# Sum of squares of x for the RMS norm factor: eight strip products on TensorE replaced by three adds on VectorE and one product with ones

## The chip, the cores and the metric

One Trainium2 chip (trn2), one of its NeuronCores. The metric is the device time of one execution in microseconds (us); for several executions their median is given. TensorE multiplies matrices and writes PSUM, VectorE (DVE in the rows) and ScalarE (ACT) do elementwise work, SyncE (SP) starts the DMAs that bring the weights. The engines run side by side and wait for one another through semaphores; each works through its own instructions in program order.

## The reference, cut to what matters

Two transformer blocks (`l` = 0, 1) are followed by a modulated attention and retention layer and a mixture of experts. All is float32, 256 tokens of width 1024. In each of the two blocks an RMS norm stands at three places:

```python
def rms_norm(x, g):
    xf = x.astype(jnp.float32)
    y = xf * lax.rsqrt(jnp.mean(xf * xf, axis=-1, keepdims=True) + EPS)
    return (y * g.astype(jnp.float32)).astype(x.dtype)
...
    for l in range(DEPTH):
        h = rms_norm(x, norm_g[l, 0])
        x = x + 0.5 * swiglu(h, ffn_w_gate[l, 0], ffn_w_up[l, 0], ffn_w_down[l, 0])
        h = rms_norm(x, norm_g[l, 1])
        proj = h @ w_in[l]
        ...
        h = rms_norm(x, norm_g[l, 2])
        x = x + 0.5 * swiglu(h, ffn_w_gate[l, 1], ffn_w_up[l, 1], ffn_w_down[l, 1])
```

The change is about how `jnp.mean(xf * xf)` is formed at these six places (two blocks with three norms each).

## The kernel before

x is held turned: `xT` has 128 partitions, eight tiles (`KD`), and 256 tokens in each. A tile is 128 of the 1024 features, so the sum over features runs over eight tiles and over the 128 partitions. The products with x don't wait for the norm: they take x times the gain, rounded into `hh` (high part) and `hl` (rest), and the result is multiplied afterwards with the factor 1/rms of each token (`rstd`). A weight comes in pieces of 128x1024 by DMA into `W`; ScalarE makes its high part `WH` (L1522), VectorE its rest `WL` (L1907), four pairs in rotation (`PAIRS`), and TensorE makes three products for each 128x128 weight (`mm3`, L799, recorded at L780).

The norm factor is made while TensorE already works at the first two blocks of the products. ScalarE squares x into `mT` (L1545, four instructions of two tiles). TensorE, after the first block of products (the gate block of an FFN, or block c = 0 of the projection), does `squares_by_strip` (L872): each of the eight tiles of squares is multiplied with 32 columns of ones, tile k into the strip of 32 partitions at k % 4 * 32 of PSUM bank 0, so that four strips each hold the sum of two tiles. ScalarE copies the strips to `rs` (`strips_out`, L1548, recorded at L1551). TensorE, after the second block of products, does `squares_of_strips` (L881): ones times `rs`, which adds all partitions; every row of a strip counts 32 times, hence the scale 1/(32 D). ScalarE takes the root (`root`, L1553, recorded at L1556), VectorE the reciprocal (`norm_factor`, L1958, recorded at L1961), and then the results of the first blocks are multiplied with it.

The order of the work around this is written out by hand, engine by engine, and fixed when the kernel is built:

- TensorE, `ffn` (L936) at b = 0: gate products, strips, up products, product of the strips, then block 1. The projection (L1003 on) does the same with c = 0, c = 1 and c = 2.
- ScalarE: `used(2)` (L1525) makes the high parts of the pieces due next; in `ffn` (L1624) two such calls, `strips_out` and `root` stand ahead of the first Silu.
- VectorE: `used(2)` (L1910) makes the rests; in `ffn` (L2145) and in the projection (L2210 on) two such calls stand ahead of `norm_factor` at b = 0 or c = 0.

A piece may be split ahead of its use by three pieces, as far as a pair is free:

```python
                while may_split(st["split"], st["used"], free, ahead):
                    n = st["split"]
                    dve.wait_ge(high_ready, n + 1)
                    ...
                    v.tensor_tensor(low, W[:, i % RAW, :], high.bitcast(F32), ALU.subtract).then_inc(low_ready, 1)
```

With pieces 0 and 1 for the first block of products and 2 and 3 for the second, the first `used(2)` reaches piece 4 and the second one piece 6. Piece 6 takes the pair of piece 2, so its high part waits (`pair_used`) until TensorE is in the second half of the second block.

`link` (L1895) lets a VectorE instruction count a semaphore up and has VectorE wait for it, so that the next one reads finished data.

Of the kernel before, what the change touches and what calls it, by code (L numbers as in the profile page):

```python
# [8 lines left out]
ALU = mybir.AluOpType  # L9
ACT = mybir.ActivationFunctionType  # L10
# [8 lines left out]
T = 256  # L19
# [259 lines left out]
def build(nc, I, out):  # L279
    ctx = ExitStack()  # L280
    with ctx:
# [492 lines left out]
        def _(pe):  # L774
# [94 lines left out]
                       f == 0, f == 1, then=work_ready if f else None)  # L869
                turns.step()  # L870

            def squares_by_strip():  # L872

                for k in range(KD):
                    if k % 2 == 0:
                        pe.wait_ge(sq_ready, due(sq_ready))
                    at = k % 4 * 32
                    mm(ps[at:at + 32, 0, 0:T], ones[:, 0:32], mT[:, k, :], k < 4, k >= 4,
                       then=sum_ready if k == KD - 1 else None)

            def squares_of_strips():  # L881

                pe.wait_ge(part_ready, due(part_ready))
                mm(ps[:, 1, 0:T], ones[:, :], rs[:, :], True, True, then=sum_ready)

# [50 lines left out]
            def ffn(l, i):  # L936

                for b in range(FF_BLOCKS + 1):
                    if b < FF_BLOCKS:
                        two_tiles("ffn_gate", begin(), h_wait=b == 0, then=work_ready)  # L940
                        turns.step()
                        if b == 0:
                            squares_by_strip()
                        two_tiles("ffn_up", begin(), then=work_ready)
                        turns.step()
                        if b == 0:
                            squares_of_strips()
                    if (l, i, b) == (0, 0, LATE_BLOCK):
                        late_vectors()
                    if ada_unit(l, i, b) is not None:  # L950
                        if ada_unit(l, i, b) == 0:
                            pe.wait_ge(act_setup, 3)
                        if ada_unit(l, i, b) < SUMMED_FROM:
                            ada_rows(ada_unit(l, i, b))
                    if ada_unit(l, i, b - 1) is not None:
                        ada_columns(ada_unit(l, i, b - 1))
                    if (l, i, b) == (1, 1, CONTEXT_AT + 1):
                        turn_context()
                    if (l, i, b) == (1, 1, CONTEXT_AT + 2):
                        pe.wait_ge(lrow_ready, 1)  # L960
                        bank = begin()
                        mm(bank[:, 0:40], ones[0:1, :], lrow[:, :], True, True, then=work_ready)
                        turns.step()
                    if 0 < b < FF_BLOCKS:
                        c = b - 1
                        pe.wait_ge(hid_ready, due(hid_ready))
                        for f in range(2):
                            w = take("ffn_down")
                            hid = at((hid_h[:, c % 2, :], hid_l[:, c % 2, :]), f * T, T)
                            for n in range(KD):  # L970
                                mm3(ps[:, n // 2, (n % 2) * T:(n % 2 + 1) * T], at(w, n * P), hid,
                                    c == 0 and f == 0 and n % 2 == 0, False)
                            done_pair()
                pe.wait_ge(hid_ready, due(hid_ready))
                c = FF_BLOCKS - 1
                ws = [take("ffn_down") for f in range(2)]
                for n in range(KD):
                    for f in range(2):
                        hid = at((hid_h[:, c % 2, :], hid_l[:, c % 2, :]), f * T, T)
                        mm3(ps[:, n // 2, (n % 2) * T:(n % 2 + 1) * T], at(ws[f], n * P), hid, False, f == 1,  # L980
                            then=acc_ready if f and n % 2 == 1 else None)
                done_pair(2)
# [20 lines left out]
            for l in range(DEPTH):  # L1003
                ffn(l, 0)
                proj = {}
                for c in range(15):
                    bank = begin()
                    if c not in (4, 5, 10, 11, 14):
                        two_tiles("w_in", bank, h_wait=c == 0, then=work_ready)
                    else:  # L1010

                        for half in range(2):
                            w = take("w_in")
                            for j in range(4):
                                k = 4 * half + j
                                end = k == KD - 1
                                if c == 14:
                                    mm3(bank[:, 0:T], at(w, j * 256), h_at(k), k == 0, end)
                                n, v0 = (P, T) if c == 14 else (256, 0)
                                for tt in range(TT):  # L1020
                                    mm3(bank[:, v0 + tt * n:v0 + (tt + 1) * n], h_at(k, tt * P, P),
                                        at(w, j * 256 + 256 - n, n), k == 0 and tt == 0 and c != 14, end,
                                        then=work_ready if end and tt else None)
                            done_pair()
                    proj[c] = turns.step()
                    if c == 0:
                        squares_by_strip()
                    if c == 1:
                        squares_of_strips()
                    if c == 2:  # L1030
                        turn_factor(l)

# [470 lines left out]
        def _(act):  # L1503
# [41 lines left out]
                    nc.scalar.activation(mT[:, 2 * b:2 * b + 2, :], xT[:, 2 * b:2 * b + 2, :], ACT.Square)\  # L1545
                        .then_inc(sq_ready, 1)

            def strips_out():  # L1548

                act.wait_ge(sum_ready, due(sum_ready))  # L1550
                nc.scalar.activation(rs[:, :], ps[:, 0, 0:T], ACT.Copy).then_inc(part_ready, 1)  # L1551

            def root():  # L1553

                act.wait_ge(sum_ready, due(sum_ready))
                nc.scalar.activation(rs[:, :], ps[:, 1, 0:T], ACT.Sqrt, bias=eps[:, :], scale=1.0 / (32 * D))\  # L1556
                    .then_inc(rms, 1)

            def split_to(n):
# [64 lines left out]
            def ffn(l, i):  # L1624
                for b in range(FF_BLOCKS):
                    used(2)
                    if (l, i, b) == (0, 0, LATE_BLOCK + 1):
                        set_up()
                    if b == 0:
                        used(2)  # L1630
                        strips_out()
                        root()
                    act.wait_ge(work_free, turns.n + 1)
                    nc.scalar.activation(sg[:, b % 2, :], sg[:, b % 2, :], ACT.Silu).then_inc(sg_ready, 1)
                    turns.step()
                    if b:
                        used(2)
                    turns.step()
                    if (l, i, b) == (0, 0, LATE_BLOCK):
                        turns.step(LATE_TURNS)  # L1640
                    turns.step((ada_unit(l, i, b) is not None and ada_unit(l, i, b) < SUMMED_FROM) +
                               (ada_unit(l, i, b - 1) is not None))
                    if (l, i, b) == (1, 1, CONTEXT_AT):
                        context_root()
                    if (l, i, b) == (1, 1, CONTEXT_AT + 1):
                        round_context()
                        turns.step()
                    if (l, i, b) == (1, 1, CONTEXT_AT + 2):
                        turns.step()
                    if b:  # L1650
                        used(2)
                turns.step(ada_unit(l, i, FF_BLOCKS - 1) is not None)
                used(2, ahead=PAIRS - 2)
# [20 lines left out]
            for l in range(DEPTH):  # L1674
# [3 lines left out]
                for c in range(15):  # L1678
                    used(2)
                    act.wait_ge(work_ready, turns.n + 1)  # L1680
                    turns.step()
                    if c == 0:
                        strips_out()
                    if c == 1:
                        root()
                for s in range(MIX_STEPS):
# [184 lines left out]
        def _(dve):  # L1871
# [80 lines left out]
            def mixed_low(k):  # L1952
# [2 lines left out]
                v.tensor_tensor(mix_l[:, k, :], mT[:, k, :], mix_h[:, k, :].bitcast(F32), ALU.subtract)\  # L1955
                    .then_inc(mix_low, 1)

            def norm_factor():  # L1958

                dve.wait_ge(rms, due(rms))  # L1960
                v.reciprocal(rstd[:, :], rs[:, :]).then_inc(rstd_ready, 1)  # L1961
                dve.wait_ge(rstd_ready, due(rstd_ready))
# [182 lines left out]
            def ffn(l, i):  # L2145
                for b in range(FF_BLOCKS):
                    used(2)
                    if b == 0:
                        used(2)
                        norm_factor()  # L2150
                    bank = take()
                    give(v.tensor_tensor(by_two(sg[:, b % 2, :]), by_two(bank), factor_by_two(), ALU.mult))
# [57 lines left out]
            for l in range(DEPTH):  # L2210
# [4 lines left out]
                for c in range(15):  # L2215
# [3 lines left out]
                        used(2)  # L2219
                    if c == 0:  # L2220
                        used(2)
                        norm_factor()
                    bank = take()
                    if c == 4:
# [576 lines left out]
```

## Time and profile before

| | us |
|---|---|
| median of 3 runs | 1992.77 |
| lowest and highest | 1991.96, 1993.86 |
| profiled execution, its own time | 1993.51 |
| its span in the profile | 1991.7 |
| TensorE busy (matmuls) | 1940.5 (97%) |
| VectorE busy | 1223.4 (61%) |
| ScalarE busy | 703.2 (35%) |

The span runs from the first to the last instruction of the profiled execution; its own time is 1.8 us longer. Matmuls overlap in the pipeline, so that the distance from start to start is what one costs and not the duration in its row. The mean granted TensorE clock was 0.994 of full speed.

### The profile page before, as it was taken

The page shows a single profiled execution, that of the slowest core. Times are in us where ns is not written, and L with a number is a line of the kernel's source. Part 1 is how long each engine was busy: PE and PEld are TensorE (multiplying, and loading weights), DVE is VectorE, ACT ScalarE, POOL GpSimd, SP SyncE. Part 2 cuts the span into 40 slices and gives each one's busy share as a digit, 9 for nine tenths or more (in the row PEclk, how much of TensorE's full clock was granted, in tenths as well). Part 3 has the DMA queues.
Part 4 walks back from the last instruction along what each step waited for, and adds up shares of the span by engine and source line. Part 5 has one row for each costly group of instructions (what it writes and reads, how often), then busy time and mean ns, then how long its engine had stood idle before and what let it go on. Part 6 is the DMA issues. An engine that isn't in the chain of part 4 may idle for free.

```text
span 1991.7 us, 33632 instructions
## 1 busy us (share of the span) xinstructions
PE 1940.5 (97%) x14053; PEld 1598.8 (80%) x14053; DVE 1223.4 (61%) x2117; ACT 703.2 (35%) x1052; POOL 0.2 (0%) x4
## 2 busy tenths in 40 slices
PE   9999999999999999999999999999898999999997
PEld 9999998889999999999888999999665444434432
DVE  6665759877567877775987777757766333222221
ACT  5433536535334543353653534343332000000001
POOL 0000000000000000000000000000000000000000
PEclk9999999999999999999999999999899999999999
DMA  7798563276776677656325675654309999999996
GB/s 238 240 346 267 174 189 117 96 204 207 224 221 203 212 233 228 200 182 185 117 96 180 206 239 185 197 121 128 127 22 340 421 421 421 421 422 421 421 421 280
DMA packets 275282, 476.66 MB, mean 239 GB/s; under 512 B 29254, under 2 KB 235136, under 8 KB 250552
## 3 DMA queue, kind: packets, MB, share of 16 engines
q1 hardware_dynamic: 274876, 474.38, 68.9%
q8 instruction: 114, 1.87, 0.4%
q14 instruction: 40, 0.33, 0.1%
q10 hardware_dynamic: 252, 0.08, 0.0%
HBM read 473.27 MB, written 7.95 MB: 242 GB/s over the span
## 4 chain that ended last, share of the span: by engine, by line
PE 82%; DMA 11%; DVE 5%; ACT 1%; SPq 1%; issue 1%; DVEq 0%; ACTq 0%
PE ps L780 80%; DMA ring_over<-in_moe_w_up_dram 4%; DMA ring_zone<-in_moe_w_up_dram 3%; DMA hl_place<-in_moe_w_gate_dram 1%; DMA hl_place<-in_moe_w_up_dram 1%; DMA hT<-in_moe_w_up_dram 1%; SPq L700 1%; PE ps L1120 1%; PE ps L1263 0%; DVE PT L2353 0%; DVE WL L1978 0%; PE ps L1440 0%; DVE hl L1918 0%; ACT mT L1758 0%; ACT gT L1706 0%
## 5 line engine op out<-in xcount | busy, mean ns | idle before, releaser
L780 PE MATMUL ps<-hh,WH 128*128 128x256 f32 x2232 | 633.1, 284 | 1.3 <-DVE WL L1907 0.7
L780 PE MATMUL ps<-hl,WH 128*128 128x256 f32 x2232 | 622.9, 279 | 0.0
L780 PE MATMUL ps<-hh,WL 128*128 128x256 f32 x2232 | 622.9, 279 | 0.0
L1907 DVE TENSOR_TENSOR WL<-W,WH 128x1024 fp32r<-128x1024 f32 x390 | 471.6, 1223 | 244.0 <-ACT WH L1522 242.4
L1522 ACT ACTIVATE WH<-W 128x1024 fp32r<-128x1024 f32 x390 | 408.2, 1055 | 434.1 <-PE ps L780 398.2
L780 PEld LDWEIGHTS ps<-hh,WH 128*128 128x128 f32 x2232 | 418.8, 188 | 14.8 <-issue 11.6
L780 PEld LDWEIGHTS ps<-hl,WH 128*128 128x128 f32 x2232 | 418.7, 188 | 1.2 <-issue 1.0
L780 PEld LDWEIGHTS ps<-hh,WL 128*128 128x128 f32 x2232 | 418.8, 188 | 0.0
L780 PE MATMUL ps<-hid_h,WH 128*128 128x256 f32 x704 | 200.6, 285 | 0.0
L780 PE MATMUL ps<-hid_l,WH 128*128 128x256 f32 x704 | 197.6, 281 | 0.0
L780 PE MATMUL ps<-hid_h,WL 128*128 128x256 f32 x704 | 197.3, 280 | 0.0
L1838 ACT ACTIVATE sgE<-ps 128x512 f32<-128x512 f32 x16 | 9.6, 597 | 433.0 <-PE ps L780 433.0
L780 PEld LDWEIGHTS ps<-hid_h,WH 128*128 128x128 f32 x704 | 133.2, 189 | 3.5 <-issue 3.3
L2733 DVE TENSOR_TENSOR hidE<-sgE,ps 128x512 f32<-128x512 f32 x16 | 16.7, 1043 | 190.8 <-PE ps L780 190.8
L780 PEld LDWEIGHTS ps<-hid_l,WH 128*128 128x128 f32 x704 | 133.1, 189 | 0.0
L780 PEld LDWEIGHTS ps<-hid_h,WL 128*128 128x128 f32 x704 | 133.0, 189 | 0.0
L780 PE MATMUL ps<-yT,W 128*128 128x256 f32 x512 | 117.0, 381 | 0.8 <-DVE yT L2466 0.4
L780 PE MATMUL ps<-ring_over,XT 128*64 128x512 f32 x432 | 109.9, 594 | 6.7 <-DMA ring_over<-in_moe_w_up_dram 5.4
L780 PEld LDWEIGHTS ps<-yT,W 128*128 128x128 f32 x512 | 94.6, 190 | 15.7 <-issue 2.8
L780 PE MATMUL ps<-ring_zone,XT 128*64 128x512 f32 x336 | 89.1, 594 | 9.7 <-DMA ring_zone<-in_moe_w_up_dram 4.6
L780 PEld LDWEIGHTS ps<-ring_over,XT 128*64 128x64 f32 x432 | 37.6, 137 | 67.0 <-issue 66.9
L2750 DVE TENSOR_TENSOR yS<-ps,xT 128x512 f32<-128x512 f32 x32 | 22.1, 692 | 89.8 <-PE ps L780 89.8
(401 smaller groups left out, 2601.8 us busy)
## 6 DMA issues: line engine op xcount, KB each, us to landing
W<-in_ffn_w_gate_dram SPq DMA_DIRECT2D x88, 512.0 KB, 5.2
W<-in_ffn_w_up_dram SPq DMA_DIRECT2D x88, 512.0 KB, 4.8
W<-in_ffn_w_down_dram SPq DMA_DIRECT2D x88, 512.0 KB, 3.9
W<-in_w_in_dram SPq DMA_DIRECT2D x78, 512.0 KB, 4.6
ring_over<-in_moe_w_up_dram SPq DMA_DIRECT2D x28, 1024.0 KB, 26.5
ring_over<-in_moe_w_down_dram SPq DMA_DIRECT2D x28, 1024.0 KB, 26.2
ring_over<-in_moe_w_gate_dram SPq DMA_DIRECT2D x26, 1024.0 KB, 25.5
W<-in_w_gate_dram SPq DMA_DIRECT2D x48, 512.0 KB, 4.5
```

Of the source, the lines that this page charges most:

```text
L700: sp.dma_start(tile.rearrange("p (k n) -> p k n", k=src.shape[1]), src).then_inc(loaded, 16)
L780: ins = nc.tensor.matmul(o, lhsT, rhs, start=start, stop=stop, skip_group_check=True, **kw)
L1120: ins = nc.tensor.transpose(ps[:, TURN_BANK, k * T + q * P:k * T + (q + 1) * P], S[:, u % 4, q * T + k * P:q * T + (k + 1) * P], ident)
L1522: nc.scalar.activation(high, W[:, i % RAW, :], ACT.Copy).then_inc(high_ready, 1)
L1838: nc.scalar.activation(sgE[:, :], bank, ACT.Silu).then_inc(sg_ready, 1)
L1907: v.tensor_tensor(low, W[:, i % RAW, :], high.bitcast(F32), ALU.subtract).then_inc(low_ready, 1)
L2733: v.tensor_tensor(hidE[:, :].rearrange("p (k m) -> p m k", k=HIDDEN), by_row(sgE[:, :]), by_row(bank), ALU.mult).then_inc(work_free, 2)
L2750: give(v.tensor_tensor(yS[:, half * 512:(half + 1) * 512], bank, gate_rows[:, half * 512:(half + 1) * 512], ALU.mult))
```

## The change

VectorE adds the squares over the tiles in place in `mT`: 1024 columns (tiles 0 to 3 and 4 to 7), then 512, then 256 into `rs`. TensorE does the one product with ones, ScalarE takes the root with scale 1/D. Gone are the strip products and the copy of the strips. The adds stand on VectorE where `norm_factor` stood, directly ahead of it; the product stands on TensorE where `squares_of_strips` stood.

```diff
--- before.py
+++ after.py
@@ -869,17 +869,9 @@
                        f == 0, f == 1, then=work_ready if f else None)
                 turns.step()
 
-            def squares_by_strip():
-
-                for k in range(KD):
-                    if k % 2 == 0:
-                        pe.wait_ge(sq_ready, due(sq_ready))
-                    at = k % 4 * 32
-                    mm(ps[at:at + 32, 0, 0:T], ones[:, 0:32], mT[:, k, :], k < 4, k >= 4,
-                       then=sum_ready if k == KD - 1 else None)
-
-            def squares_of_strips():
-
+            def sum_of_squares():
+
+                due(sq_ready, 4)
                 pe.wait_ge(part_ready, due(part_ready))
                 mm(ps[:, 1, 0:T], ones[:, :], rs[:, :], True, True, then=sum_ready)
 
@@ -939,12 +931,10 @@
                     if b < FF_BLOCKS:
                         two_tiles("ffn_gate", begin(), h_wait=b == 0, then=work_ready)
                         turns.step()
-                        if b == 0:
-                            squares_by_strip()
                         two_tiles("ffn_up", begin(), then=work_ready)
                         turns.step()
                         if b == 0:
-                            squares_of_strips()
+                            sum_of_squares()
                     if (l, i, b) == (0, 0, LATE_BLOCK):
                         late_vectors()
                     if ada_unit(l, i, b) is not None:
@@ -1023,10 +1013,8 @@
                                         then=work_ready if end and tt else None)
                             done_pair()
                     proj[c] = turns.step()
-                    if c == 0:
-                        squares_by_strip()
                     if c == 1:
-                        squares_of_strips()
+                        sum_of_squares()
                     if c == 2:
                         turn_factor(l)
 
@@ -1545,15 +1533,10 @@
                     nc.scalar.activation(mT[:, 2 * b:2 * b + 2, :], xT[:, 2 * b:2 * b + 2, :], ACT.Square)\
                         .then_inc(sq_ready, 1)
 
-            def strips_out():
+            def root():
 
                 act.wait_ge(sum_ready, due(sum_ready))
-                nc.scalar.activation(rs[:, :], ps[:, 0, 0:T], ACT.Copy).then_inc(part_ready, 1)
-
-            def root():
-
-                act.wait_ge(sum_ready, due(sum_ready))
-                nc.scalar.activation(rs[:, :], ps[:, 1, 0:T], ACT.Sqrt, bias=eps[:, :], scale=1.0 / (32 * D))\
+                nc.scalar.activation(rs[:, :], ps[:, 1, 0:T], ACT.Sqrt, bias=eps[:, :], scale=1.0 / D)\
                     .then_inc(rms, 1)
 
             def split_to(n):
@@ -1628,7 +1611,6 @@
                         set_up()
                     if b == 0:
                         used(2)
-                        strips_out()
                         root()
                     act.wait_ge(work_free, turns.n + 1)
                     nc.scalar.activation(sg[:, b % 2, :], sg[:, b % 2, :], ACT.Silu).then_inc(sg_ready, 1)
@@ -1679,8 +1661,6 @@
                     used(2)
                     act.wait_ge(work_ready, turns.n + 1)
                     turns.step()
-                    if c == 0:
-                        strips_out()
                     if c == 1:
                         root()
                 for s in range(MIX_STEPS):
@@ -1955,6 +1935,14 @@
                 v.tensor_tensor(mix_l[:, k, :], mT[:, k, :], mix_h[:, k, :].bitcast(F32), ALU.subtract)\
                     .then_inc(mix_low, 1)
 
+            def sum_over_tiles():
+
+                dve.wait_ge(sq_ready, due(sq_ready, 4))
+                squares = flat(mT[:, :, :])
+                link(v.tensor_tensor(squares[:, 0:4 * T], squares[:, 0:4 * T], squares[:, 4 * T:8 * T], ALU.add))
+                link(v.tensor_tensor(squares[:, 0:2 * T], squares[:, 0:2 * T], squares[:, 2 * T:4 * T], ALU.add))
+                v.tensor_tensor(rs[:, :], squares[:, 0:T], squares[:, T:2 * T], ALU.add).then_inc(part_ready, 1)
+
             def norm_factor():
 
                 dve.wait_ge(rms, due(rms))
@@ -2147,6 +2135,7 @@
                     used(2)
                     if b == 0:
                         used(2)
+                        sum_over_tiles()
                         norm_factor()
                     bank = take()
                     give(v.tensor_tensor(by_two(sg[:, b % 2, :]), by_two(bank), factor_by_two(), ALU.mult))
@@ -2219,6 +2208,7 @@
                         used(2)
                     if c == 0:
                         used(2)
+                        sum_over_tiles()
                         norm_factor()
                     bank = take()
                     if c == 4:
```

## Rows read from the trace of the kernel before

**Rows 1.** The profile page: chain that ended last, shares of the span by engine

```profile
PE 82%; DMA 11%; DVE 5%; ACT 1%; SPq 1%; issue 1%; DVEq 0%; ACTq 0%
```

**Rows 2.** The same chain in order of time: start, us, what; two pieces

```profile
39.57 267.17 PE ps L780 x2296
...
426.14 527.08 PE ps L780 x4442
```

**Rows 3.** Timeline of TensorE around the strips (start, us, ...)

```profile
20.52 0.28 PE L780 MATMUL ps<-hh,WL 128*128 128x256 f32 x1
20.73 1.07 PE L780 MATMUL ps<-mT,ones 128*32 128x256 f32 x16
21.73 0.39 PE L780 MATMUL ps<-hh,WH 128*128 128x256 f32 x1
```

**Rows 4.** Timeline of TensorE around the product of the strips

```profile
27.49 0.59 PE L780 MATMUL ps<-rs,ones 128*128 128x256 f32 x2
```

**Rows 5.** Timeline of ScalarE in the same stretch

```profile
25.04 1.06 ACT L1522 ACTIVATE WH<-W 128x1024 fp32r<-128x1024 f32 x1 [2.54 <-PE ps L780]
...
26.39 1.28 ACT L1556 ACT_TABLE_LOAD   x1
```

**Rows 6.** Timeline of VectorE in the same stretch

```profile
26.13 1.23 DVE L1907 TENSOR_TENSOR WL<-W,WH 128x1024 fp32r<-128x1024 f32 x1 [2.37 <-ACT WH L1522]
28.63 1.75 DVE L1961 RECIPROCAL rstd<-rs 128x256 f32<-128x256 f32 x1 [1.27 <-ACT rs L1556]
...
31.88 0.69 DVE L2161 TENSOR_TENSOR S<-S 128x512 f32<-128x512 f32 x1 [0.17 <-ACT S L1634]
32.60 0.43 DVE L2162 CAST hid_h<-S 128x512 fp32r<-128x512 f32 x1
```

**Rows 7.** VectorE and TensorE at the second norm of block 0 (projection)

```profile
222.24 1.23 DVE L1907 TENSOR_TENSOR WL<-W,WH 128x1024 fp32r<-128x1024 f32 x1 [1.55 <-ACT WH L1522]
223.59 0.59 PE L780 MATMUL ps<-rs,ones 128*128 128x256 f32 x2
```

**Rows 8.** VectorE and TensorE at the last norm of block 1

```profile
1127.94 1.23 DVE L1907 TENSOR_TENSOR WL<-W,WH 128x1024 fp32r<-128x1024 f32 x1 [1.61 <-ACT WH L1522]
...
L780 PE MATMUL ps<-rs,ones x2: 378/378/378, 1129.3 to 1129.5; 128*128 128x256 f32 x2
```

**Rows 9.** Adds of 128x256 by tile: ns min/median/max, first and last start

```profile
L2275 DVE TENSOR_TENSOR mT<-mT,rs x32: 424/425/426, 411.6 to 1094.8; 128x256 f32<-128x256 f32 x32
```

**Rows 10.** The reciprocal's line, same columns

```profile
L1961 DVE RECIPROCAL rstd<-rs x6: 1752/1753/1754, 28.6 to 1130.4; 128x256 f32<-128x256 f32 x6
```

**Rows 11.** Timeline: TensorE waits for a rest made by VectorE

```profile
16.43 2.35 DVE L1907 TENSOR_TENSOR WL<-W,WH 128x1024 fp32r<-128x1024 f32 x2
...
17.71 0.39 PE L780 MATMUL ps<-hh,WH 128*128 128x256 f32 x1 [0.68 <-DVE WL L1907]
17.93 0.28 PE L780 MATMUL ps<-hl,WH 128*128 128x256 f32 x1
18.05 0.28 PE L780 MATMUL ps<-hh,WL 128*128 128x256 f32 x1
```

**Rows 12.** TensorE after three idle stretches, from the timeline

```profile
1233.45 1.23 PE L780 MATMUL ps<-WR,MOD 128*1 128x40 f32 x16 [4.37 <-DVE gT L2006]
...
1397.77 0.35 PE L780 MATMUL ps<-WH,hc_h 128*128 128x256 f32 x1 [2.33 <-DVE S L2370]
...
1543.92 0.66 PE L1440 MATMUL ps<-C,hidE 128*128 128x128 f32 x4 [3.06 <-DVE hidE L2733]
```

**Rows 13.** Windows of TensorE: stretch, sum, busy (instructions), granted clock, DMA share, GB/s

```profile
1234.00:1235.00 1.00, 1.00 (x13) 0.50 0.00 0
...
1239.00:1240.00 1.00, 1.00 (x10) 0.97 0.00 0
...
1395.00:1400.00 5.00, 2.67 (x21) 1.00 0.64 206
...
1545.00:1550.00 5.00, 4.34 (x22) 1.00 1.01 419
```

## The prediction, made before the changed kernel had run

> **What bounds the kernel now.** I read the chain that ended last first, then the same chain in order of time, then the timeline of each engine around one of the norms, and last the clock. The chain is TensorE for 82% of the span, and DMA for 11% [rows 1]. In order of time the stretches in which the six norms lie are unbroken TensorE: 267 us from 39.57 on and 527 us from 426.14 on [rows 2]. So what is taken from TensorE in these stretches is gained, and what TensorE has to wait for is lost; work of ScalarE or VectorE counts only where TensorE waits for it. The six norms are the six reciprocals [rows 10]. The profiled execution took 1993.51 us with a span of 1991.7 us; the median of the runs is 1992.77 us, and I add the difference worked out below to the median.
>
> **Removed from TensorE: the strips.** The last product before them starts at 20.52, the first after them at 21.73 [rows 3]; in an unbroken row they start 0.12 us apart, as at 17.93 and 18.05 [rows 11]. The strips cost 21.73 - 20.52 - 0.12 = 1.09 us. Six times that is 6.5 us off the path, the whole of what the change can gain. The copy of the strips on ScalarE is 0.4 us beside TensorE's work and is worth nothing: the load of the root's table that follows it starts at 26.39 and is done at 27.67, before the product of the strips has ended, and without the copy it only starts sooner [rows 4, 5]. In the projection the root stands behind a wait for the second block of products before and after, so nothing moves there.
>
> **Added on TensorE: nothing.** The product with ones and `rs` has the same shape as that of the strips and stands in the same place.
>
> **Added on VectorE: three adds, and where they stand.** This is the step that decides. The adds are ahead of the reciprocal and behind two `used(2)`, in VectorE's program order. The last rest made there is that of piece 6, and it runs from 26.13 to 27.36 [rows 6]. It can't be sooner: it waited 2.37 us for its high part, which started at 25.04 after waiting 2.54 us for TensorE, since piece 6 takes over the pair of piece 2 [rows 5, 6]. TensorE frees that pair as it enters the second half of the second block. So the start of this rest is tied to TensorE's own progress, and taking out the strips moves both sooner by the same 1.09 us. The squares have been ready for long (ScalarE's four squares lie before the strips), but the adds can't use that, as they stand behind this rest.
>
> TensorE reached the product of the strips at 27.49, 1.36 us after the start of that rest [rows 4, 6]. At the second norm it is 223.59 - 222.24 = 1.35 us [rows 7], at the last one 1129.3 - 1127.94 = 1.36 us [rows 8]; the other three read the same. All six are one case.
>
> No row shows an add of 128x1024 in place. The nearest is the rest itself, two inputs and 1024 columns: 1.23 us [rows 6]. For 512 columns it is L2161, 0.69 us [rows 6], for 256 the add of `mT` and `rs`, 0.425 us [rows 9]. They fit one line (0.266 us for 256 columns, 0.54 for 512), so I take them as they are. A pair of rests takes 2.35 us and not 2.46 [rows 11], so that an instruction with no wait on the one before it starts 1.13 us after that one's start: the first add starts at 26.13 + 1.13 = 27.26 on the old scale. Linked instructions start 32.60 - 31.88 = 0.72 us apart where the first one lasts 0.69 [rows 6], which is 0.03 for a link. The sum: 27.26 + (1.23 + 0.03) + (0.69 + 0.03) + 0.425 = 29.67. From the end of a rest, 16.43 + 1.23 = 17.66, to the product that waited for it, 17.71, is 0.05 [rows 11], so TensorE starts its product with ones at 29.72 in place of 27.49: it stands still for 2.23 us. Then it starts cold: 17.93 - 17.71 = 0.22 where it is otherwise 0.12 [rows 11], 0.10 more. In all 2.33 us lost.
>
> The Trainium skill (VectorE: DVE Perf Modes, The DRAIN you can't avoid) says that the next VectorE operation starts only once the pipe of the one before it is empty, whether or not a semaphore lies between. By that rule the first add would start at the end of the rest, 27.36, and the sum would be 0.1 us larger for each norm, 0.6 us in all. The pair of rests in 2.35 us [rows 11] speaks against it for two independent operations, and I stay with the rows.
>
> **What waits behind.** While VectorE adds, what is queued behind the adds is the reciprocal and, behind it, the products with the factor. The reciprocal waited 1.27 us for the root in any case [rows 6], and the root waits for TensorE's product. Both keep their distance from TensorE's product, which restarts the whole group at once; so no second wait follows, and later rests aren't later as TensorE sees it. The DMA queue only gets ahead during the stall. The same holds for the high parts on ScalarE, which wait for TensorE.
>
> **The sum.** 2.33 - 1.09 = 1.24 us for each norm, times six is 7.4 us: 1993.51 + 7.4 = 2000.9 for an execution like the profiled one, and 1992.77 + 7.4 = 2000.2 as a median. After the last norm the delay isn't made up, since the products that follow are in the same chain, and the loads of the experts go into places that earlier work has to free.
>
> **Bounds.** From below: if each add gives up 0.1 us to the next, as unlinked instructions do, and there is no cold start, a norm costs 2.33 - 0.3 - 0.1 - 1.09 = 0.84 us, 5.0 in all: 1997.8. From above: if each of the three hand-overs takes 0.17 us, the idle time that L2161 shows behind ScalarE [rows 6], in place of 0.03 to 0.05, and the first add starts at the end of the rest, it is 1.24 + 0.4 + 0.1 = 1.74 us, 10.4 in all: 2003.2.
>
> **Rivals.** (1) **Faster: the adds are hidden.** If the adds were done before TensorE comes to its product, all that is left is the gain, 6.5 us: 1986.3. VectorE was idle for 2.37 us before the rest of piece 6 [rows 6], just the 2.4 us that the adds need, so they would fit if they ran there. It decides whether they stand ahead of that rest or behind it; the point is an end of the adds before 27.49 on the old scale. The order of the code is against it: both `used(2)` come first. 6 in 100. (2) **No difference: the stall is made up.** DMA is 11% of the chain, at its end [rows 1]. If the loads of the experts started by a time that TensorE doesn't set, the delay would vanish there: 1992.8. The order of the kernel speaks against it. Adds at half the durations taken would end there too, with a stall of 1.1 us; the rest of 1.23 us speaks against that. 10 in 100 together. (3) **Much slower: the clock falls.** After an idle stretch of 4.37 us TensorE's clock was at 0.50 of full speed (the lower of its two levels, 1.2 of 2.4 GHz), and back at 0.97 in the window from 1239 [rows 12, 13]. Work from 1233.45 to about 1239.1 then ran at half speed, which cost 2.8 us. Six such falls would give 2000.2 + 17 = 2017. But after idle stretches of 2.33 and of 3.06 us the clock stayed at 1.00 [rows 12, 13], and the stall forecast here is 2.2 us. 4 in 100. The Trainium skill (TensorE: Matmul & The Clock Gate, Why this matters for your kernels) warns of idle gaps between bursts for this very reason; the trace agrees for the longest gap and shows none for the two shorter ones.
>
> **How the numbers follow.** The forecast case has 80 in 100, at 2000.2. The range takes in its bounds, 1997.8 to 2003.2, and some 0.8 us to each side for the scatter of the runs (the three lie 1.9 us apart): 1997.0 to 2004.0. It leaves out the three rivals, 20 in 100. With 0.2% (4 us) as the bound, about what a measurement of this kernel can tell from no change: slower has the forecast and rival 3, 0.84; same has rival 2, 0.10; faster has rival 1, 0.06.
>
> **What would show it.** In the changed kernel TensorE waits six times for VectorE's `rs`, about 2.2 us each, and stands so in the list of waits with some 13 us. The strips are gone, and up products follow gate products 0.12 us apart. VectorE shows the rest of piece 6, then three adds of 1.23, 0.69 and 0.42 us with no idle time between, then an idle time of about 1.2 us before the reciprocal. The granted clock stays at 1.00 around the norms. The prediction is wrong if TensorE doesn't wait there (rival 1), if a TensorE wait or a DMA wait further on has shrunk by the same amount (rival 2), if the clock falls behind the stalls (rival 3), or if the wait is there with another length, which means an add or a hand-over was mis-sized.

## The result, and the profile after

The changed kernel took 2009.21 us (median of 4 runs, 2006.32 to 2012.25), the kernel before 1992.77 us (median of 3) in the same comparison. Medians are of fast executions: one of the kernel before took 2879.39 us here, another 11020.75 us beside the second set of experiments, and neither is counted. The ratio is 1.0083, with a 95% interval of 1.0071 to 1.0095. So it is slower, as forecast, but by 16.4 us and not by 7.4, and outside the range of 1997.0 to 2004.0.

The profiled execution took 2012.25 us with a span of 2010.5 us, 18.8 us more than the span before, and its mean granted clock was 0.990 (0.994 before). The chain that ended last, from the page of the changed kernel:

```profile
PE 79%; DMA 10%; DVE 6%; ACT 2%; SPq 2%; issue 1%; DVEq 0%; ACTq 0%
```

TensorE has 3% of the chain less than before and DMA 1% less; VectorE, ScalarE and SyncE's queue have 1% more each [rows 1]. Who TensorE waited for, from the list of waits (waiter, whom for, us in total, times, longest):

```profile
PE ps L780 <- DVE rs L1944: 14.5, 6, 4.1
...
PE ps L780 <- DVE WL L1887: 3.3, 6, 0.7
```

The first line is the stall that the prediction named: six times, 14.5 us in all, against a forecast of 13. The second stood in the list of the kernel before with a single wait of 0.7 us; five of its six are new. Both lines can be read in one norm, that of the projection of block 0. TensorE of the changed kernel at the end of the first block and of the second (start, us, engine, ...):

```profile
221.34 0.28 PE L780 MATMUL ps<-hh,WL 128*128 128x256 f32 x1
222.15 0.36 PE L780 MATMUL ps<-hh,WH 128*128 128x256 f32 x1 [0.53 <-DVE WL L1887]
...
227.76 0.28 PE L780 MATMUL ps<-hh,WL 128*128 128x256 f32 x1
230.13 0.70 PE L780 MATMUL ps<-rs,ones 128*128 128x256 f32 x2 [2.08 <-DVE rs L1944]
```

and VectorE in the same stretch:

```profile
220.78 4.63 DVE L1887 TENSOR_TENSOR WL<-W,WH 128x1024 fp32r<-128x1024 f32 x4 [2.50 <-ACT WH L1510]
226.53 1.23 DVE L1887 TENSOR_TENSOR WL<-W,WH 128x1024 fp32r<-128x1024 f32 x1 [1.12 <-ACT WH L1510]
227.67 1.22 DVE L1942 TENSOR_TENSOR mT<-mT 128x1024 f32<-128x1024 f32 x1
228.92 0.69 DVE L1943 TENSOR_TENSOR mT<-mT 128x512 f32<-128x512 f32 x1
229.65 0.42 DVE L1944 TENSOR_TENSOR rs<-mT 128x256 f32<-128x256 f32 x1
```

The second block of products can't start before the rest of piece 2 is there, the first of the four at 220.78, done at 222.0. TensorE was through with the first block at 221.6 and waited. In the kernel before, the same four rests started at the same place in the work, and this is what TensorE and VectorE did then:

```profile
216.06 4.63 DVE L1907 TENSOR_TENSOR WL<-W,WH 128x1024 fp32r<-128x1024 f32 x4 [2.50 <-ACT WH L1522]
...
216.62 0.28 PE L780 MATMUL ps<-hh,WL 128*128 128x256 f32 x1
216.83 1.07 PE L780 MATMUL ps<-mT,ones 128*32 128x256 f32 x16
217.83 0.39 PE L780 MATMUL ps<-hh,WH 128*128 128x256 f32 x1
```

The rest of piece 2 was done at about 217.3, under the strips. So the strips covered a wait: from the last product to the first of the next block it is 217.83 - 216.62 = 1.21 us with them and 222.15 - 221.34 = 0.81 us without. They were worth 0.40 us at this norm and not 1.09. At the other four new waits the same distance gives 0.47, 0.20, 0.47 and 0.47 us, and at the first norm, where no wait is new, 1.09. Together that is 3.1 us and not 6.5.

The third part is the clock. Windows of TensorE in the changed kernel (stretch, length, busy, granted clock, DMA share, GB/s), the first four around four of the norms, the last three inside the fourth:

```profile
20.00:40.00 20.00, 15.91 (x113) 0.83 0.65 203
215.00:235.00 20.00, 17.39 (x144) 1.00 0.43 141
470.00:500.00 30.00, 27.46 (x217) 0.94 0.49 159
870.00:900.00 30.00, 27.45 (x215) 0.94 0.49 148
...
884.00:885.00 1.00, 1.00 (x8) 0.94 0.97 306
885.00:888.00 3.00, 3.00 (x16) 0.50 0.04 10
888.00:889.00 1.00, 1.00 (x9) 0.85 0.00 0
```

At three of the six stalls the clock went to its lower level of 1.2 GHz for a while (20 us times 0.17 missing is 3.4 us of full-speed time, 30 us times 0.06 is 1.8, twice), about 7 us in all for this execution. The other three norms stayed at 1.00. The stalls were equal in length at five of the norms, 2.1 us; the clock fell behind two of these five and not behind three.

The clock also fell behind two stalls that the change doesn't touch, those of 2.33 and 3.06 us, which had left it at 1.00 in the kernel before [rows 12, 13]. In the changed kernel:

```profile
1413.34 0.36 PE L780 MATMUL ps<-WH,hc_h 128*128 128x256 f32 x1 [2.33 <-DVE S L2360]
...
1414.00:1417.00 3.00, 3.00 (x16) 0.50 0.49 161
...
1563.78 0.82 PE L1428 MATMUL ps<-C,hidE 128*128 128x128 f32 x4 [3.06 <-DVE hidE L2723]
...
1564.00:1567.00 3.00, 2.76 (x12) 0.52 1.02 426
```

So the same stall can pass in one execution and bring the clock down in another.

The first norm had a stall of its own kind. ScalarE, VectorE and TensorE there, from the timelines:

```profile
25.03 1.06 ACT L1510 ACTIVATE WH<-W 128x1024 fp32r<-128x1024 f32 x1 [3.77 <-DMA W<-in_ffn_w_up_dram]
...
26.12 1.22 DVE L1887 TENSOR_TENSOR WL<-W,WH 128x1024 fp32r<-128x1024 f32 x1 [3.61 <-ACT WH L1510]
27.26 1.22 DVE L1942 TENSOR_TENSOR mT<-mT 128x1024 f32<-128x1024 f32 x1
28.51 0.69 DVE L1943 TENSOR_TENSOR mT<-mT 128x512 f32<-128x512 f32 x1
...
29.72 1.22 PE L780 MATMUL ps<-rs,ones 128*128 128x256 f32 x2 [4.09 <-DVE rs L1944]
```

The high part of piece 6 started at 25.03, as before [rows 5], but now it waited for its weights and not for TensorE. TensorE had come 0.8 us sooner from its start in this execution and 1.1 us sooner by the strips, and both were lost here, in a stall of 4.1 us. How late these weights are differs between executions: against the stall of the second norm, that of the first is 2.0 us longer here, 0.4 us longer with the stall filled (0.67 and 0.30 us), and no longer with two adds (0.83 and 0.82). These two are experiments below that have no strips either.

### The profile page after: what moved, and what is told of

It reads as the page before. It is cut to its first block, busy times and chain, and to the rows that moved or that the text cites. A ratio compares the mean times of both kernels' runs of the same rounds, so it can differ in the third digit from the quotient of the medians.

```text
span 2010.5 us, 33450 instructions
## 1 busy us (share of the span) xinstructions
PE 1943.7 (97%) x13957; PEld 1601.3 (80%) x13957; DVE 1237.5 (62%) x2135; ACT 702.0 (35%) x1046; POOL 0.2 (0%) x4
## 4 chain that ended last, share of the span: by engine, by line
PE 79%; DMA 10%; DVE 6%; ACT 2%; SPq 2%; issue 1%; DVEq 0%; ACTq 0%
PE ps L780 78%; DMA ring_over<-in_moe_w_up_dram 3%; DMA ring_zone<-in_moe_w_up_dram 3%; DMA hl_place<-in_moe_w_gate_dram 1%; DMA hl_place<-in_moe_w_up_dram 1%; DMA hT<-in_moe_w_up_dram 1%; SPq L700 1%; PE ps L1108 1%; DVE WL L1887 1%; ACT WH L1510 1%; ACT mT L1533 0%; PE ps L1251 0%; DVE xT L1905 0%; DVE mT L1942 0%; DVE PT L2343 0%
```

## The experiments

The theory: the adds cost because they stand behind the rest of piece 6; the strips had covered a wait; and the stall brings the clock down. The rivals: the adds cost by their load on VectorE alone; the strips were worth 1.09 us; the clock falls for some other reason. Eight runs were made in two sets, each set on one chip beside runs of the kernel before (median 1992.64 us in the first, 1993.4 us in the second).

**The adds sooner.** In `ffn`, and in the same way at c = 0 of the projection:

```diff
                     if b == 0:
-                        used(2)
                         sum_over_tiles()
+                        used(2)
                         norm_factor()
```

> The three adds stand ahead of the second used(2) on VectorE, so ahead of the rests of pieces 5 and 6; all else is the changed kernel. Theory A (the stall of 2.1 us comes from the adds standing behind the rest of piece 6, and the lower clock follows from the stall): the six waits for rs vanish, the falls of the clock at the norms too, and what is left is the gain on the strips less the wait of 0.5 us for a rest that the strips had covered, some 0.5 us for each norm: 1989 to 1991 us, 2 to 4 us below the kernel before. Theory B (the adds cost by their mere load on VectorE, 2.3 us each norm, wherever they stand): still 2000 us or more.

Measured: 1987.78 us, ratio to before 0.9974 (0.9965 to 0.9984); again in the second set 1987.23 us, 0.9973 (0.9963 to 0.9983). That is 21 us below the changed kernel, and 4.9 and 6.2 us below the kernel before, a little more than the 2 to 4 expected. The rows give 3.1 us for the strips, and the spans of the profiled executions lie 3.6 and 4.2 us below that of the kernel before; the 2 to 3 us by which the medians exceed the rows aren't explained. VectorE at the projection norm of block 0, and TensorE's waits:

```profile
217.89 1.22 DVE L1942 TENSOR_TENSOR mT<-mT 128x1024 f32<-128x1024 f32 x1
219.14 0.69 DVE L1943 TENSOR_TENSOR mT<-mT 128x512 f32<-128x512 f32 x1
219.87 0.42 DVE L1944 TENSOR_TENSOR rs<-mT 128x256 f32<-128x256 f32 x1
220.21 2.35 DVE L1887 TENSOR_TENSOR WL<-W,WH 128x1024 fp32r<-128x1024 f32 x2
...
PE ps L780 <- DVE WL L1887: 3.0, 6, 0.7
```

The same three adds with the same durations now run while TensorE is in its second block, no wait for `rs` is left, and the two rests behind them come late enough to do no harm. The clock was at 1.00 in windows around all six norms. So VectorE's load is not what cost the time; its order is. The wait for WL is still there.

**The strips kept.** The changed kernel, with strip products put back that nobody reads:

```diff
+            def strips():
+
+                for k in range(KD):
+                    at = k % 4 * 32
+                    mm(ps[at:at + 32, 0, 0:T], ones[:, 0:32], hh[:, k, :].bitcast(F32), k < 4, k >= 4)
+
...
                         turns.step()
+                        if b == 0:
+                            strips()
                         two_tiles("ffn_up", begin(), then=work_ready)
...
+                    if c == 0:
+                        strips()
                     if c == 1:
                         sum_of_squares()
```

> The changed kernel with the sixteen strip instructions put back at their old place, as work whose result nobody reads (they multiply the rounded x in place of the squares, since VectorE adds in place there). Theory A (in the kernel before the strips partly covered a wait for the rest of piece 2, so they were worth 0.5 us a norm and not 1.09): 2 to 3 us above the changed kernel, and its waits of 0.5 us for WL ahead of the second block are gone. Theory B (they were worth their full 1.09 us, as forecast): 6.5 us above the changed kernel.

Measured: 2011.09 us (2010.47 to 2014.94, 4 runs), ratio to before 1.0092 (1.0077 to 1.0107): 1.9 us above the changed kernel, by medians of different sets whose runs of before agree within 0.1 us. The waits, and the clock behind four of the six stalls:

```profile
PE ps L780 <- DVE rs L1954: 12.5, 6, 2.1
...
PE ps L780 <- DVE WL L1897: 0.7, 1, 0.7
...
31.00:34.00 3.00, 3.00 (x17) 0.51 0.10 28
492.00:495.00 3.00, 3.00 (x16) 0.50 0.08 28
885.00:887.00 2.00, 2.00 (x9) 0.50 0.35 120
1148.00:1150.00 2.00, 2.00 (x10) 0.50 0.16 54
```

The five waits for WL are gone, as they are hidden again. The difference of 1.9 us is known only to some 4 us, by the intervals of the two ratios, and it holds what the clock did besides. It speaks against 6.5, and doesn't tell 1.9 from the 3.1 that the rows give. All six stalls are 2.1 us long in this execution, and the clock fell at the first, third, fifth and sixth norm and stayed at 1.00 at the other two.

**The stall filled.** Eight products of ones with ones ahead of the wait:

```diff
                 due(sq_ready, 4)
+                keep_busy(ps[:, 0, :], 8)
                 pe.wait_ge(part_ready, due(part_ready))
```

> The changed kernel, with eight products of ones with ones on TensorE (128 columns each, into bank 0, read by nobody) ahead of its wait for rs, so some 1.6 us of the 2.1 us stall is filled. Theory A (a good part of what is lost beyond the stalls is the lower clock that follows them): the clock stays at 1.00 around the norms, and the time falls from 2009 to 2003 to 2006 us, although TensorE gets its rs no sooner. Theory B (the clock falls for other reasons): 2009 us or more.

Measured: 2004.00 us (2001.22 to 2004.89), ratio to before 1.0056 (1.0042 to 1.0070), 5.2 us below the changed kernel. The filler at the projection norm of block 0, and two windows:

```profile
223.96 1.95 PE L780 MATMUL ps<-ones 128*128 128x128 f32 x16
226.21 0.70 PE L780 MATMUL ps<-rs,ones 128*128 128x256 f32 x2 [0.30 <-DVE rs L1945]
...
20.00:40.00 20.00, 19.34 (x167) 1.00 0.69 223
...
470.00:500.00 30.00, 29.24 (x254) 1.00 0.50 164
```

TensorE gets `rs` no sooner, only the time in between isn't idle, and the clock stays at 1.00 at all six norms. So some 5 us of the 16 are the clock's, and it is idle TensorE that brought it down. What is left, 2004.0 - 1992.6 = 11.4 us, is the stalls less the gain. The 5.2 us are the difference of two medians and hold whatever the clock did in later stretches too.

**Two adds.** The first of the three adds is taken out of `sum_over_tiles`, so that this kernel leaves tiles 4 to 7 out of the sum of squares:

```diff
-                link(v.tensor_tensor(squares[:, 0:4 * T], squares[:, 0:4 * T], squares[:, 4 * T:8 * T], ALU.add))
                 link(v.tensor_tensor(squares[:, 0:2 * T], squares[:, 0:2 * T], squares[:, 2 * T:4 * T], ALU.add))
```

> The changed kernel without the first of the three adds, so tiles 4 to 7 are left out of the sum of squares. Each stall is 1.25 us shorter, about 0.85 us in place of 2.1. Theory A (the clock fell because of the length of the stall): the clock stays at 1.00 at all six norms, so the time falls by 6 times 1.25 and by the 5 us or so of the clock, to 1996 to 1998 us. Theory B (the clock falls with any stall at this place): 2001 to 2003 us.

Measured: 1995.34 us (1993.60 to 1997.90), ratio to before 1.0012 (1.0002 to 1.0021), 0.7 us below the range expected. Its waits for `rs`, and windows around two norms:

```profile
PE ps L780 <- DVE rs L1943: 5.1, 6, 0.9
...
20.00:40.00 20.00, 19.17 (x158) 1.00 0.73 239
...
470.00:500.00 30.00, 28.61 (x247) 1.00 0.60 183
```

With stalls of 0.9 us the clock fell at none of the six norms. The time went down by 14 us, where the shorter stalls alone give 7.5; some 5 us more are the clock, by the experiment before, and 1 us is open.

**The weights first.** As with the adds sooner, and in `round_and_square` on ScalarE:

```diff
                 if early:
                     halves(free=2)
+                else:
+                    halves(free=3)
                 for b in range(4):
```

> As the kernel with the adds sooner, and ScalarE makes one high part (piece 2) ahead of the four squares at the projection norms and at the first norm of block 1, and at the last norm of each block as far as pairs are free. Theory A (the wait of 0.5 us for WL ahead of the second block comes from the high part standing behind the squares on ScalarE): this wait vanishes where the high part moves, and the time is 1 to 3 us below the kernel with the adds sooner, 1987 to 1989 us. Theory B (it is tied to something else, the DMA or a free pair): equal to that kernel within 1 us.

Measured: 1982.25 us (1981.15 to 1985.38), ratio to before 0.9948 (0.9935 to 0.9962). ScalarE and VectorE at the projection norm of block 0, and the waits:

```profile
211.06 1.04 ACT L1510 ACTIVATE WH<-W 128x1024 fp32r<-128x1024 f32 x1
212.01 2.18 ACT L1535 ACTIVATE mT<-xT 128x512 f32<-128x512 f32 x4
...
212.21 1.23 DVE L1889 TENSOR_TENSOR WL<-W,WH 128x1024 fp32r<-128x1024 f32 x1 [0.41 <-ACT WH L1510]
...
PE ps L780 <- DVE WL L1889: 0.7, 1, 0.7
```

The time is 5.5 us below the kernel with the adds sooner, more than the 1 to 3 expected. The high part of piece 2 stands ahead of the squares, its rest follows, and the wait is gone at five norms (the first norm had this order already; its one wait of 0.7 us lies at the start and was there before). From the last product of the first block to the first of the second it is 0.12 us at all six norms, so the strips' full 1.09 us are gained only now.

**The weights first, in the kernel before.** The same two lines, with strips and all else as before.

> The kernel before, strips and all, with only the reorder on ScalarE of the kernel with the weights first (high part of piece 2 ahead of the squares). Theory A (in the kernel before the strips filled this wait, so the reorder is worth something only once they are gone): 1992.6 us within 1.5 us. Theory B (the reorder gains by itself, and the 10.4 us of the kernel with the weights first are mostly its doing): 1988 us or less.

Measured: 1993.58 us (1991.69 to 1995.03, 11 runs), ratio to before 1.0001 (0.9992 to 1.0010). The reorder alone is worth nothing, since the strips filled the wait; the rows give it something to take away only once they are gone.

**The difference of the two best, once more.** Both kernels again on one chip, unchanged.

> The kernel with the adds sooner once more, beside the next one on the same chip, to set their difference on one footing: 1987 to 1989 us.

> The kernel with the adds sooner and the weights first once more. If the 5.5 us between the two are the reorder's (0.6 us at each of six norms, and what the chain makes of it), it is 3 to 6 us below the kernel with the adds sooner again; if they were one chip's scatter, within 2 us of it.

Measured: 1987.23 us (1985.6 to 1989.39) and 1985.97 us (1983.15 to 1987.29). The first is as expected; the second is only 1.3 us below it, under the 3 to 6 expected and within the 2 us that stood for scatter. So the times don't show what the reorder gains; they put it anywhere from 1.3 to 5.5 us. What the rows show is that five waits are gone, 0.62 to 0.69 us each from product to product, 3.2 us in all. The version with both has the lowest median in either set, 0.9948 and 0.9964 (0.9950 to 0.9977) of the kernel before. That is 10.4 and 7.5 us, where the rows give 6.5 for the strips.

## Why the prediction was wrong

**The mechanism was right.** The adds stand behind the rest of piece 6, that rest starts 1.1 us after TensorE's entry into the second half of the block, and TensorE waits at its product six times. The adds took 1.22, 0.69 and 0.42 us (forecast 1.23, 0.69, 0.425), the first began 227.67 - 226.53 = 1.14 us after the start of the rest (forecast 1.13); from the start of the rest to TensorE's product it is 230.13 - 226.53 = 3.60 us (forecast 29.72 - 26.13 = 3.59). The Trainium skill (VectorE: DVE Perf Modes, The DRAIN you can't avoid) has the next operation start only once the pipe is empty, but the section adds that one that isn't held back starts earlier, which the prediction left out. The trace agrees with the addition: the first add starts 0.09 us ahead of the end of the rest. VectorE waited for the root as before (1.9 us on average at the last five norms, 1.8 before); that ScalarE's copy was worth nothing was not tested by itself. The experiment with the adds sooner shows that the stall came of the order alone. Rival 1, the adds hidden, needs only one line moved; it was not what the change did.

**Failed step 1: "Removed from TensorE: the strips."** It took the whole of 1.09 us as gained, and said that taking out the strips moves TensorE and the rest both sooner by that. Measured is 1.21 - 0.81 = 0.40 us at a norm of the projection, since TensorE then waits 0.53 us for the rest of piece 2 and starts cold. The strips had hidden this wait, and the list of waits of the kernel before could not show it. It could have been found there all the same: in that kernel VectorE's four rests start at 216.06 and the first is done at 216.06 + 1.23 = 217.29, while without the strips TensorE would want it 0.12 us after its last product, at 216.74. The term was put at 6.5 us and measured 3.1, which is 3.4 less. With it the sum is 7.4 + 3.4 = 10.8 us, and the filled stall, which has no loss of clock at the norms, measured 11.4.

**Failed step 2: the clock, left out of the sum and given to rival 3 alone.** The prediction gave it 4 in 100, on the ground that stalls of 2.33 and 3.06 us had left the clock at 1.00, and priced it as six falls or none. What happened lies between: falls at three norms of six in the profiled execution, worth about 5 us by the filled stall, and about 1.7 us for each fall of 3.4 us at half speed (forecast 2.8). Two rows without a fall were taken for a safe length; they showed only that a stall of that length may pass. The same two stalls, of 2.33 and 3.06 us, were both followed by the lower clock in the changed kernel.

**The sum, as the runs have it:** from the last product to the product with ones it is 230.13 - 227.76 = 2.37 us and not 0.12, so a stall costs 2.25 us, and the cold start behind it 0.1, as forecast. Six times 2.35 is 14.1 us, less 3.1 for the strips gives 11.0; the filled stall measured 11.4. The clock adds 5.2, the difference from the filled stall to the changed kernel. Together that is 16.2 us by the terms; measured are 16.4 us in the comparison of the two. The profiled execution has 2 to 3 us more, in part by its first norm, where the weights came late. In part it may be the low clock in later, thinly filled stretches, which the kernel before has too but less of; how often either comes was not tried.

## What to carry to other kernels

Work moved from a full engine to an idle one is free only if it is queued where that engine is idle: here the place of one line, in two functions, decided between 16 us lost and 5 to 6 us gained. Before work on the critical engine is counted as gain, look at when its next input is ready and not only at the list of waits, since the work may cover a wait that has no row yet. And a stall repeated on TensorE should be priced with its clock: here stalls of 0.9 us cost nothing by it, and those of 2.1 us did at some places. One trace without a fall doesn't show that a length is safe.

## What the runs showed of the hardware

- Equal stalls of 2.1 us in an otherwise full TensorE were followed by the lower clock at two of five norms in the changed kernel and at four of six with the strips kept; stalls of 0.9 us, and stalls of 2.1 us filled with products that nobody reads, at none of six. What decides which of the equal stalls is followed by a fall was not tested.
- A later stall of 2.33 us that all these kernels share left the clock at 1.00 in the kernel before and brought it to 0.50 in the changed one; so did one of 3.06 us (0.52).
- After such a fall TensorE ran at 0.50 of full speed for about 3.4 us (3 us in the window from 885 on, and the 0.1 and 0.3 us that the windows beside it lack). Behind the stall of 4.37 us, which both kernels have, it lasted until about 1239 in the kernel before, from 1234 at the latest [rows 12, 13]. In the changed kernel the stall ends at 1250.42, and the clock is 0.52 in the window from 1250 to 1253 and 1.00 from 1254 to 1257. So one length of stall was followed by stretches of different length.
- The first add of a chain starts 0.09 us before the end of the independent rest ahead of it, while linked adds start 0.03 to 0.04 us after one another's end.
